# Squares summed on VectorE before one product with ones, a conditioning vector formed earlier in a tile, and weight tiles that share transfers

## The reference

```
x = x + y                                                   # layer i of the first block
h = rms_norm(x, norm_mlp[i])
x = x + square(relu(h @ w_mlp_up[i])) @ w_mlp_down[i]        # 1024 -> 4096 -> 1024
x = x + (p[i] @ w_ple_proj[i]) * sigmoid(x @ w_ple_gate[i])  # 256 -> 1024 and 1024 -> 1024
...
mod = silu(c) @ w_ada + b_ada                               # third block: 6 x 1024 numbers
...                                                         # conv branch: layer norm, silu, @ w_conv_pw
y_rwkv = (...) @ w_o
x = x + gate1 * (merged @ w_out)
h2 = modulate(rms_norm(x, g_norm2), shift2, scale2)
x = x + gate2 * (square(relu(h2 @ w_ff1)) @ w_ff2)
return rms_norm(x, g_final)
```

## Time and profile before

| what | value |
|---|---|
| median of 3 runs | 3665.07 us (3653.8 to 3669.39) |
| profiled execution, its own time | 3657.74 us |
| its span in the profile | 3655.9 us |
| TensorE busy | 3305.3 us, 90% of the span |
| VectorE busy | 2015.0 us, 55% |
| ScalarE busy | 1299.8 us, 36% |
| GpSimd busy | 374.7 us, 10% |
| mean granted TensorE clock | 0.950 |
| transfers | 274.78 MB, mean 75 GB/s |

### The profile page before, as it was taken

How to read it: one execution, slowest core, us unless ns; L and a number is a source line. 1 busy time by engine, 2 the same in 40 slices (tenths; PEclk the granted TensorE clock), 3 DMA queues, 4 the chain that set the end, 5 groups by cost and what they waited for, 6 DMA issues and landing times.

```text
span 3655.9 us, 51894 instructions
## 1 busy us (share of the span) xinstructions
PE 3305.3 (90%) x21498; PEld 2605.7 (71%) x21498; DVE 2015.0 (55%) x3571; ACT 1299.8 (36%) x2143; POOL 374.7 (10%) x334
## 2 busy tenths in 40 slices
PE   6898899999899999998986889879999889989998
PEld 4667777777585677777765666567777777768886
DVE  5455356653432466654555437678778762554443
ACT  3234232222223342223333135456555533323221
POOL 0001000000000000000001000055445420000000
PEclk9899899999898999999997989989999989999999
DMA  3220023442551124432310220221111102233231
GB/s 126 61 69 2 24 93 128 132 133 68 85 99 42 37 96 138 138 115 69 127 46 26 62 87 12 75 61 39 45 41 40 45 5 87 81 110 104 93 99 62
DMA packets 318856, 274.78 MB, mean 75 GB/s; under 512 B 10912, under 2 KB 310048, under 8 KB 317856
## 3 DMA queue, kind: packets, MB, share of 16 engines
q1 hardware_dynamic: 314368, 256.07, 23.2%
q10 hardware_dynamic: 4256, 15.40, 1.1%
HBM read 265.16 MB, written 6.29 MB: 74 GB/s over the span
## 4 chain that ended last, share of the span: by engine, by line
PE 76%; DVE 13%; ACT 6%; issue 3%; POOL 1%; DMA 1%; DVEq 0%; ACTq 0%; SPq 0%; POOLq 0%
PE ps L95 74%; DVE f L107 4%; DVE f L101 3%; DVE r L101 3%; ACT f L88 2%; PE ps L98 2%; ACT f L92 1%; ACT r L92 1%; DVE f L104 1%; ACT f L89 1%; ACT L88 1%; POOL f L101 1%; DVE f L113 1%; DVE f L110 1%; DMA f<-in_w_in_odd 0%
## 5 line engine op out<-in xcount | busy, mean ns | idle before, releaser
L95 PE MATMUL ps<-r,r 128*128 128x512 f32 x10368 | 2459.2, 396 | 124.8 <-DVE r L101 87.3
L95 PEld LDWEIGHTS ps<-r,r 128*128 128x128 f32 x10368 | 1925.1, 190 | 601.7 <-issue 182.9
L95 PE MATMUL ps<-f,f 64*64 64x64 f32 (+9 forms) x10192 | 809.2, 270 | 181.2 <-ACT f L92 45.9
L101 DVE TENSOR_TENSOR r<-f,r 128x1024 fp32r<-128x1024 f32 (+2 forms) x621 | 657.4, 1064 | 461.7 <-ACT r L92 454.1
L95 PEld LDWEIGHTS ps<-f,f 64*64 64x64 f32 (+3 forms) x10192 | 601.7, 157 | 363.0 <-issue 168.8
L92 ACT ACTIVATE r<-f 128x1024 fp32r<-128x1024 f32 (+2 forms) x548 | 506.6, 937 | 783.4 <-PE ps L95 661.1
L101 POOL TENSOR_TENSOR f<-f,f 128x256 f32<-128x256 f32 (+1 forms) x276 | 331.3, 1213 | 478.5 <-ACT f L88 267.7
L107 DVE SCALAR_TENSOR_TENSOR f<-f,f,f 128x128 f32<-128x128 f32 (+3 forms) x622 | 365.7, 593 | 26.5 <-ACT f L88 7.3
L101 DVE TENSOR_TENSOR f<-ps,f 128x512 f32<-128x512 f32 (+7 forms) x333 | 180.4, 554 | 339.5 <-PE ps L95 329.9
L92 ACT ACTIVATE f<-ps 128x256 f32<-128x256 f32 (+3 forms) x422 | 183.7, 451 | 512.9 <-PE ps L95 364.9
L88 ACT ACTIVATE f<-ps 128x512 f32<-128x512 f32 (+3 forms) x203 | 112.0, 553 | 621.5 <-PE ps L95 619.4
(11 more groups left out here) (33 smaller groups left out, 733.3 us busy)
## 6 DMA issues: line engine op xcount, KB each, us to landing
f<-in_w_mlp_up SPq DMA_DIRECT2D x32, 1024.0 KB, 6.0
f<-in_w_mlp_down SPq DMA_DIRECT2D x32, 1024.0 KB, 6.1
f<-in_w_ff SPq DMA_DIRECT2D x32, 1024.0 KB, 5.2
f<-in_w_ada SPq DMA_DIRECT2D x48, 512.0 KB, 3.9
f<-in_w_in SPq DMA_DIRECT2D x24, 1024.0 KB, 5.0
f<-in_w_in SPq DMA_DIRECT2D x44, 512.0 KB, 3.6
f<-in_w_in_even SPq DMA_DIRECT2D x12, 1024.0 KB, 5.2
f<-in_w_in_odd SPq DMA_DIRECT2D x12, 1024.0 KB, 12.8
```

The lines of the kernel that those rows point to most:

```text
L95: return self.e.matmul(out, l, r, start=first, stop=last)
L101: return self.e.tensor_tensor(out, a, b, op)
```

## The change

Six edits. (1) In mlp0 and mlp1 VectorE adds the squares of x into one tile `acc` (one add behind each of the tiles 2 to 8), TensorE multiplies acc once with ones behind tile 10, and VectorE forms r2 behind tile 12. (2) Within a tile of an MLP, VectorE's part of `Ada` stands behind the split of the next weights and ahead of the wait for relu or for the down result; before it stood at the tile's end. (3) `Norm` gets `held`: for norm1 of the third block and the last norm VectorE adds the squares 1 to 5 onto square 0, and TensorE multiplies three times (the sum, 6 and 7) behind tile 7 of the product in front. (4) third.mu and third.var become one product each, with VectorE adding the tiles before, in the place of seven products; third.var stands one tile earlier. (5) `piece` joins up to 2048 numbers per partition, and four weights are kept as one object, so that w_ple_gate, w_conv_pw_3 and w_rwkv_o_3 go by two tiles in a transfer, w_ple_proj by eight, and the second w_out product by four: 302 rows on SyncE in place of 334. (6) w_in_odd is stored with 120 more columns of zeros, 4224 in place of 4104, which no product reads.

```diff
@@ Weights.piece
-        if g and len(g) == 1 and kind == "w" and kts * w <= 1024:
-            q = self.pieces[g[0]]
+        if g and kind == "w" and kts * w * (len(g) + 1) <= 2048:
+            q = self.pieces[g[-1]]
@@ Norm.sum_pe
-        if kt == 0:
+        if self.held and kt < 5:
+            return
+        first = kt == (5 if self.held else 0)
+        if first:
             self.bank = K.ps.hold(pe, ("rms_root", self.r + 1))
             pe.wait_ge("d_head", 32)
-        pe.wait_ge("rms_sqa" if kt % 2 else "rms_sqd", 4 * self.r + kt // 2 + 1)
-        t = pe.mm(K.ps.t[self.bank][:, :], self.weight(kt), K.h[:, kt, :], kt == 0, kt == 7)
+        if self.held and kt == 5:
+            pe.wait_ge("rms_acc", self.a0 + 5)
+            kt = 0
+        else:
+            pe.wait_ge("rms_sqa" if kt % 2 else "rms_sqd", 4 * self.r + kt // 2 + 1)
+        t = pe.mm(K.ps.t[self.bank][:, :], self.weight(kt), K.h[:, kt, :], first, kt == 7)
@@ Norm.square_dve
+        if self.held and kt >= 3:
+            j, h = kt - 2, self.K.h
+            dve.wait_ge("rms_sqa" if j % 2 else "rms_sqd", 4 * self.r + j // 2 + 1)
...
+            dve.tt(h[:, 0, :], h[:, 0, :], h[:, j, :], ADD).then_inc(self.K.S("rms_acc"), 1)
@@ Mlp.pe
-                if up and g == 0 and self.gain is not None:
-                    if n == 0:
-                        self.bank = K.ps.hold(pe, ("mlp_var", self.n_norm + 1))
-                    else:
-                        self.square(pe, n - 1)
-            if up and g == 0 and self.gain is not None:
-                self.square(pe, 7)
-                K.ps.leave(self.bank)
+                if up and g == 1 and n == 2 and self.gain is not None:
+                    pe.wait_ge("mlp_acc", 7 * self.n_norm + 7)
+                    b = self.bank = K.ps.take(pe, ("mlp_var", self.n_norm + 1))
+                    K.mm_done(pe.mm(K.ps.t[b][:, :], K.ones, self.acc, True, True), (self.name, "norm"))
@@ Mlp.dve
                 if up:
                     G.dve(dve, (self.name, "up", g, n))
+                    self.beside_dve(dve, n)
...
                     G.dve(dve, k)
+                    self.beside_dve(dve, n)
                     dve.wait_ge("mm", K.done[k])
...
-                self.beside_dve(dve, n)
-            if up and g == 0 and self.gain is not None:
-                r2 = self.r2
...
+                if up and self.gain is not None and 2 <= 8 * g + n <= 8:
+                    self.add_square(dve, 8 * g + n - 1)
+                if up and g == 1 and n == 4 and self.gain is not None:
+                    r2 = self.r2
...
@@ Third.pe
-        for n in range(8):
-            t = pe.mm(K.ps.t[b][:, :], K.ones, self.cv[:, n, :], n == 0, n == 7)
-        K.mm_done(t, "third.mu")
+        pe.wait_ge("th_ms", 7)
+        K.mm_done(pe.mm(K.ps.t[b][:, :], K.ones, self.tmp[0], True, True), "third.mu")
...
-            if n == 3:
+            if n == 2:
                 b = self.bank["var"] = K.ps.take(pe, ("th_root", 1))
-                for j in range(8):
-                    pe.wait_ge("th_sq", j + 1)
-                    K.mm_done(pe.mm(K.ps.t[b][:, :], K.ones, self.sq[:, j, :], j == 0, j == 7), ("third.var", j))
+                pe.wait_ge("th_vs", 7)
+                K.mm_done(pe.mm(K.ps.t[b][:, :], K.ones, self.sq[:, 0, :], True, True), "third.var")
@@ arrays_of
+    arr["w_in_odd"] = np.ascontiguousarray(np.pad(I["w_in_odd"], ((0, 0), (0, 0), (0, 120))))
```

More of the change, by code:

```diff
@@ L435, with __init__ @@
 class Norm:
-    def __init__(self, K, gain, x_done, dst=None, shift=None, first=False, early=False):
+    def __init__(self, K, gain, x_done, dst=None, shift=None, first=False, early=False, held=False):
+        self.held, self.a0 = held, K.counts.setdefault("rms_acc", 0)
+        K.counts["rms_acc"] += 5 if held else 0
         self.K, self.gain, self.x_done, self.dst, self.shift = K, gain, x_done, dst, shift
@@ L1810, in act @@
                 if g == 0 and self.gain is not None:
-                    if n >= 2:
-                        act.wait_ge("mm", K.done[self.name, "norm", n - 2])
-                    act.f(self.sq[n % 2], K.x[:, n, :], ACT.Square).then_inc(S("mlp_sq"), 1)
+                    if n >= 3:
+                        act.wait_ge("mlp_acc", 7 * self.n_norm + n - 2)
+                    act.f(self.sq[n % 2] if n else self.acc, K.x[:, n, :], ACT.Square).then_inc(S("mlp_sq"), 1)
     def dve(self, dve):
@@ L1851, in dve @@
                         ahead_dve(dve, self.after, n)
-                self.beside_dve(dve, n)
-            if up and g == 0 and self.gain is not None:
-                r2 = self.r2
[L1855 to L1858, removed]
+                if up and self.gain is not None and 2 <= 8 * g + n <= 8:
+                    self.add_square(dve, 8 * g + n - 1)
+                if up and g == 1 and n == 4 and self.gain is not None:
+                    r2 = self.r2
+                    dve.wait_ge("mm", K.done[self.name, "norm"])
+                    dve.ts(r2, K.ps.t[self.bank][:, :], 1.0 / 1024, K.c("eps"), MUL, ADD).then_inc(S("mlp_var"), 1)
+                    dve.wait_ge("mlp_var", self.n_norm + 1)
+                    dve.own(dve.recip(r2, r2))
     def beside_dve(self, dve, n):
@@ L1872, in __init__ @@
         self.K, self.i, self.x_before = K, i, x_done
+        self.W_gate, self.W_proj = K.A["w_ple_gate"][i], K.A["w_ple_proj"][i]
         K.top = 512
@@ L1889, in pe @@
         for n in range(8):
-            G.tile(pe, ("ple.gate", i, n), K.A["w_ple_gate"][i], n * 128, 128, self.X, [("ple_gate", 8 * i + n + 1)])
+            G.tile(pe, ("ple.gate", i, n), self.W_gate, n * 128, 128, self.X, [("ple_gate", 8 * i + n + 1)])
             if self.mem and n > 1:
@@ L1893, in pe @@
         for n in range(8):
-            G.tile(pe, ("ple.proj", i, n), K.A["w_ple_proj"][i], n * 128, 128, self.P, [("ple_mul", 8 * i + n + 1)], kts=2)
+            G.tile(pe, ("ple.proj", i, n), self.W_proj, n * 128, 128, self.P, [("ple_mul", 8 * i + n + 1)], kts=2)
             ahead_pe(pe, self.after, n)
@@ L2235, in __init__ @@
         K.top = 512
-        self.norm = Norm(K, K.pv(name), x_done, dst=K.x, early=early)
+        self.norm = Norm(K, K.pv(name), x_done, dst=K.x, early=early, held=early)
         self.x_done = self.norm.out_done
@@ L3650, in __init__ @@
         self.out = OutProj(K, "third.out", K.A["w_out_3"][0], self.XO, lambda j: ("d_back2", 16), gate=mod[:, 16:24])
-        self.norm1 = Norm(K, gs[:, 8:16], self.out.x_done, shift=mod[:, 24:32], early=True)
+        self.norm1 = Norm(K, gs[:, 8:16], self.out.x_done, shift=mod[:, 24:32], early=True, held=True)
         self.out.after = self.norm1
@@ L3704, in act @@
             G.act(act, k)
-            for j in range(3 * n, min(3 * n + 3, 8)):
+            for j in range(4 * n, min(4 * n + 4, 8)):
                 act.wait_ge("th_td", j + 1)
                 act.f(self.sq[:, j, :], self.cv[:, j, :], ACT.Square).then_inc(S("th_sq"), 1)
-            if n == 3:
-                act.wait_ge("mm", K.done["third.var", 7])
+            if n == 2:
+                act.wait_ge("mm", K.done["third.var"])
                 act.wait_ge("th_td", 8)
@@ L3751, in dve @@
                     dve.tt(c, c, K.rinv, SUB).then_inc(S("th_td"), 1)
+            elif n == 1:
+                for j in range(1, 8):
+                    dve.wait_ge("th_sq", j + 1)
+                    dve.wait_ge("th_vs", j - 1)
+                    dve.tt(self.sq[:, 0, :], self.sq[:, 0, :], self.sq[:, j, :], ADD).then_inc(S("th_vs"), 1)
         dve.wait_ge("th_root", 1)
```

27 lines of the change are left out of this document (19 added, 8 removed).

## The result

| | median | runs |
|---|---|---|
| before | 3667.23 us | 3653.8 to 3673.52 |
| after | 3606.12 us | 3595.51 to 3612.52 |

The ratio on record is 0.9848, with a 95% interval of 0.9827 to 0.9868: faster, by 56 us of 3667 (48 to 63). The two medians shown lie 61.1 us apart, which is inside that interval. The forecast was 3607 us. The profiled execution has a span of 3593.7 us against 3655.9, 62.2 us less, where the sum said 54.7. So the time was right, and some terms were not.

A forecast was written before the change was run, and what follows sets the result against it. TensorE was taken to bound the kernel, holding 76% of the chain. Gains of 30.5 (MLPs), 6.8 (fox), 5.4 (norms) and 12.0 (third.mu, third.var) sum to 54.7 us, giving 3607 us, the middle of 3603 and 3610; range 3588 to 3631.

The forecast's parts named there:

- Up 0: Up 0 of mlp0 and mlp1: products with ones and their waits go, adds cost nothing; 9.7 us gained per MLP.
- r2: Behind tile 12 of mlp0 and mlp1: r2 delays the split for tile 14 by 1.5 us; 1.65 us lost per MLP.
- `Ada` ahead of the relu work: Up tiles of mlp0 and mlp1: twelve stalls for VectorE's split vanish, nothing replacing them; 8.1 us gained per MLP.
- fox: Turn from ple0 to fox: earlier issue hides w_in_odd's first transfer, gaining 6.8 us; padding adds nothing.
- Held norms: norm1 of the third block and last norm: 4.5 us saved, 1.8 us returned each; 5.4 us gained for both.
- third.mu and third.var: Third block: seven products of each go, with the adds covered on VectorE; 12.0 us gained.
- Cover in up 0: Up 0 of mlp0 and mlp1: with the adds, VectorE's split still ends 0.5 us before TensorE wants it.
- A: Up tiles: the split stays late and the stall moves with `Ada`; without 16 us of gain, 3623 us; chance 0.10.
- B: r2 costs 4.1 us per MLP, held norms give only 2 us, third.var loses 2 us; 3617 us; chance 0.07.
- C: Turn to fox: joined transfers do not remove the wait, so 6.8 us stay; 3614 us; chance 0.03.
- D: MLP tiles: late w_ada slices delay VectorE, then TensorE, making the kernel slower, 3740 us; chance 0.03.
- E: Behind tile 13: new 1.5 us gaps slow TensorE, up to 5.4 us each, 11 us; 3618 us; chance 0.02.

The follow-up runs named there:

- the kernel with r2 in pieces: Changed kernel with r2's reciprocal cut into four pieces behind tiles 12 to 15 and held norms adding squares 1 to 6: 3587.65 us (0.9803), again 3593.29 us (0.9824).

## Why the prediction was right, and where not

- **Up 0.** The 9.7 us per MLP (3.4 up to tile 5, 1.8 and 4.9 for the next two pairs, by the products of `Ada` in mlp1) measured 10.0. The product behind tile 10 cost 0.90 (a pair of 12.02 to 12.03 us), as said. But part of it belongs to edit 2, which takes 1.9 us of it alone (the wait behind r2) and gives the adds their cover. Edit 1 alone is worth 4.8 us per MLP, its own product and all waits counted.
- **r2.** 1.65 was said, with the wait at tile 14 and none elsewhere. The place is right, and the wait costs 1.97; with the clock behind it mostly 3.6.
- **`Ada` ahead of the relu work** was the step that failed: 8.1 us per MLP were said, from "two down tiles ... and no gap". 12 x (12.00 - 11.13) + 9 x (11.33 - 11.13) = 12.2 were there. The size of this term was wrong by half, and its mechanism was right. A pace of 11.33 us was read as gap-free because the list of waits has nothing for it; it hid 0.2 us a pair. The list can't show it: in the profile a matmul of 128x512 lasts 0.39 us and the next one starts 0.23 us behind it, so a short wait leaves no idle time, and a longer one is listed too short (1.81 us listed at r2, 1.97 paid). The 0.2 us were taken for work, and so `Ada`'s product was taken for 0.45 us where it costs 11.13 - 2 x 5.44 = 0.25. The row of 11.36 us for 48 matmuls could have been held against 2 x 5.44 = 10.9 and asked where the rest goes. The timeline of the kernel before, at a down tile of mlp0, shows it on VectorE and on TensorE's weight loads, which stop until the split is through at 789.05 + 1.22 = 790.27 us, as it starts only after `Ada`'s sum:

```profile
788.40 0.74 DVE L107 SCALAR_TENSOR_TENSOR f<-f,f,f 128x128 f32<-128x128 f32 x2
...
789.05 1.22 DVE L101 TENSOR_TENSOR r<-f,r 128x1024 fp32r<-128x1024 f32 x1
...
790.39 1.22 PEld L95 LDWEIGHTS ps<-r,r 128*128 128x128 f32 x6 [0.35 <-issue]
```

- **fox.** 6.8 was said, by the start (3.27 us measured, 3.28 said) and by the product at full speed (1.13 against 2.07 us). 6.8 measured with either edit alone, where the clock was as before at the start of ple0, and 6.4 to 7.7 in the kernels with both. That the padding adds nothing is right beside the joined transfers. It is not right that the padding is worth nothing: alone it does the same 6.8.
- **Held norms.** 5.4 said, 5.7 measured; the root comes at 4.34 us and not 4.6.
- **third.mu and third.var.** 12.0 said, 11.97 and 12.05 measured.
- **Cover in up 0.** 0.5 us said, 0.7 to 0.9 measured.
- **The rivals.** A, B, C and D did not come: no wait in up tiles but that of r2, norms and third.var as forecast, fox's wait gone, w_ada landing in 3.8, 3.9 and 6.4 us as before. E has a true part: gaps of 1.8 us do slow TensorE, by 1.6 us at a time and not 5.4, in eight of ten. That the old gaps of 1.82 us showed nothing in two of two was too few to exclude it; in two more profiles of the old order two of four had it.

The sum of the terms as measured is 2 x (10.0 - 0.9 - 2.0 + 12.2) + 6.8 + 5.7 + 12.0 = 63 us, less 1.6 for each slow pair: 60 to 63, against 54.7. The time was nevertheless met within 1 us, and that is luck. The forecast subtracted from 3661.4 us, the middle of two values, where the median of before in the result is 3667.2, 5.8 more; and the medians lie 61.1 us apart, 6.4 more than the sum. The two errors cancel. The medians of four executions also lie some us to either side: 0.9848 and 0.9831 for the same kernel are 56 and 62 us.

## What to carry to other kernels

A pace that no listed wait disturbs is not yet the pace of the engine: compare it with the sum of its parts from a stretch where nothing else runs, or a wait that the list leaves out stays hidden and is given to an instruction. Where two edits share one engine's idle time, cost them together, since one can be the cover of the other, and don't take two gains that add for independence; and where either of two edits removes the same wait, count it once. A long VectorE instruction between the works of a tile loop should be cut to the slack of a tile, and what a sum lacks at the end should be only what the last tile brings.

## What the runs showed of the hardware

- **The granted clock after short gaps.** Behind a gap of 1.81 us the clock fell to its lower level (1.2 GHz in place of 2.4) for some 3 us in eight cases of ten, and not in the other two, with the same code around it. Eight gaps of 1.0 to 1.5 us in the kernel with edit 2 undone show none. The Trainium skill, TensorE: Matmul & The Clock Gate, Part 1, has idle time lower the clock, and says that the moment of a change varies from run to run; the runs agree with both. By what the Trainium skill says there of the idle time that it takes, gaps this short would have passed, and here eight of ten did not. How long a gap may be was not tried between 1.5 and 1.8 us.
- **The time ahead of mlp0 varies by 14.7 us with the same instructions.** In 13 profiles mlp0 starts at 479.64 to 485.08 us eight times, at 488.2 once, and at 491.76 to 494.35 four times. From 200 to 300 us the granted clock was 0.98 in the profile before and 0.92 in that with padding alone, from 300 to 400 us 0.87 and 0.82. Up to the start of mlp0 the eight early profiles have 82 to 89 us at the lower clock, and the four late ones 113 to 120. Why an execution gets the one or the other is open. Of the 5.3 us between the two profiles of the changed kernel 2.4 lie here, and 3.5 of the 6.9 between those of the kernel with r2 in pieces. So a stage tells two microseconds and a median does not.
- **Rows of 16416 bytes** (4104 floats) made the transfers of 1024 KB land in 12.8 us at the median (13.1 in the kernel with edit 2 alone), rows of 16896 bytes in 5.2 to 5.4. The Trainium skill, DMA: Bandwidth & Descriptors, "How a descriptor splits into AXI transactions", would have such rows cost a part of the beats more, 22% by the estimate of the prediction; these runs show 2.4 times. In the kernel with joined transfers alone it was 9.0 us with the same rows, so what runs beside them counts too; which part is which stays open.
